# The opening of a two-block kernel: small loads moved between queues and stages, a weight slab and two memsets moved ahead

## The chip, the cores and the metric

The kernel runs on one core of a Trainium2 chip. The metric is the device time of one execution in microseconds (us), as the median of several runs.

## What is computed

Two transformer-like blocks, one behind the other, in float32, on 512 "latent" tokens and 256 context tokens of width 1024. Only the start of the first block is touched. In the reference's words:

```python
def layer_norm(x): ...                       # over the 1024 features
def ada(cvec, w, b):                         # w: 1024 x 6144
    m = jax.nn.silu(cvec) @ w + b
    return [mi[:, None, :] for mi in jnp.split(m, 6, axis=-1)]
def modulate(x, shift, scale):
    return layer_norm(x) * (1 + scale) + shift

sh1, sc1, g1, sh2, sc2, g2 = ada(c, w_ada[l], b_ada[l])
csh1, csc1, ... = ada(c_ctx[None, :], w_ada[l], b_ada[l])
u_ctx = modulate(ctx, csh1, csc1) @ w_in[l]
u_lat = modulate(x, sh1, sc1) @ w_in[l]      # w_in: 1024 x 2064
...                                          # depthwise conv, state-space scan, Fourier
                                             # mix, pooling, w_out, norm, conv FFN, then
                                             # all of the second block
```

So before the first product with `w_in`, the tokens have to be normalised and the first 2048 columns of the modulation (`sh1`, `sc1`, for both conditioning vectors) have to be there.

## The kernel before

**Layout.** Tokens lie along the free dimension, features on the 128 partitions in 8 "k-tiles" (`KT`). A norm works on 16 tiles `u`: `u` = 0 to 7 are the latent tokens (range r = 0, 512 wide), 8 to 15 the context tokens (r = 1, 256 wide).

**Weights.** All big weights come as slabs of 1024 x 256 (1 MB) through a ring of `NS` = 4 slots, in the order of the list `stream`. SyncE (SP) issues them; slab n goes into slot n % 4 and waits until slab n - 4 is used up. "Used up" is a count of `mm_done`, raised by TensorE (PE) when a unit of products is finished (`add_slabs` holds how often for each slab), or, for the slabs of `w_in`, the count `w_lo` (`split_off`): these slabs are split into a rounded part (`high`, ScalarE, ACT, line 755) and the rest (`low`, GpSimd, POOL, line 761), and once both are made from a slab its slot is free. The first slabs are 8 of `w_ada` (the modulation, "ada slabs" 0 to 7), then `w_in` 0, two more of `w_ada`, `w_in` 1, two of `w_ada`, and so on.

**The blocks.** Every `with nc.Block()` starts and ends with a barrier of all five engines.

- Block 1 (lines 1264 to 1334): SP issues the first constants, the conditioning vectors, `x` and `ctx`, then ring slabs 0 to 3, then through `load` (1268) 34 small loads (biases, gains, conv weights) and one 896 KB load of further constant matrices (`mats`). PE transposes the tokens, VectorE (DVE) and ACT copy them out of PSUM to `xT`.
- Block 2 (`units_stage`, from line 788): the norm of the tokens, the modulation, and the products with `w_in`. SP loads `wnarrow` (a 16-column piece of `w_in`) and goes on with the ring.

**The norm with its lead.** PE sums the tokens (line 436), ACT makes the mean (489), PE spreads it over the partitions (444, "mean spread"), DVE subtracts (522), ACT squares (498), PE sums the squares (436). Between them `Lead` does the first 8 ada slabs, one at every second tile `u`: PE multiplies (`ada_slab`, 621), ACT copies the result (`ada_take`, 639), PE turns it (`ada_tiles`, 630). At u = 9 PE also transposes the small parameters (1358), which needs all small loads. ACT makes the root of the variance (482; the first of them needs an activation table load), DVE its reciprocal (516), PE spreads it (444, "rstd spread" 0 for the latent, 1 for the context tokens). DVE adds the bias to the modulation (`ada_finish`, 648 and 654). From then on each tile goes through four steps on three engines: DVE multiplies (536), ACT scales and shifts (509), DVE rounds (546, "cast"), POOL subtracts to get the rest (552, "lo tile"). The products of unit group 0, the "opening" (782), go k by k: for each k-tile two units of three products, waiting for lo tile k; first all latent ones, then the context ones. Rstd spread 1 stands on PE ahead of the first product.

**Order on the other engines.** ACT makes `high` of halves 0 and 1 and the rounded narrow piece (902) behind the last root and ahead of the first step 509. POOL does `low` of halves 0 and 1, the narrow piece's rest (886), three memsets that clear the padding of the output buffers (890: 5404, 514 and 1056 columns), then the 16 lo tiles, then further `low` halves. Every engine runs its own list in order.

## Time and profile before

| | us |
|---|---|
| median of 3 runs | 2721.28 |
| lowest and highest | 2718.79, 2722.8 |
| the profiled execution: its time, and its span | 2731.0, 2729.2 |
| PE busy in the span | 2439.9 (89%) |
| DVE, POOL, ACT busy | 1210.4, 993.8, 824.2 |
| mean granted TensorE clock (share of full) | 0.932 |

The busy lines give the sum over the span. The 40 slices of the profile's page cover 68 us each, and the row of PE begins 4, 9: the first slice holds PE at 4 tenths, the second at 9 or more. The change lies within the first slice and a half. Times inside the span are counted from its start.

### The profile page before, as it was taken

To read this page: it belongs to the slowest core of one execution; us is meant where nothing else is said; L and a number is where in the kernel's file an instruction comes from. 1 tells how busy PE (TensorE), PEld (TensorE's weight loads), DVE (VectorE), ACT (ScalarE), POOL (GpSimd) and SP (SyncE) were. 2 spreads that over 40 slices of the span, in tenths; PEclk is the share of its full clock that TensorE was granted. 3 is DMA by queue.
4 is the path that set the end of the run, shared out by engine and by line. 5 is a ranking of instruction groups with operands and counts; after the bars stand their busy time and mean duration, and the time that the engine had idled before them with its cause. 6 is when DMAs were issued, how large, how long until landed. Compare 5 with 4: busy or idle time off the path is not lost. (4 is left out here: it accounts for less than half of the span.)

```text
span 2729.2 us, 35711 instructions
## 1 busy us (share of the span) xinstructions
PE 2439.9 (89%) x14567; PEld 1977.2 (72%) x14567; DVE 1210.4 (44%) x1943; ACT 824.2 (30%) x1386; POOL 993.8 (36%) x609
## 2 busy tenths in 40 slices
PE   4997788999997998767798999999989798899998
PEld 3775465777775897654586888888876587688887
DVE  3515727756554104775615323241417653333322
ACT  3232324433334223233504111121215164322221
POOL 1434333545554331211025334342425001555553
PEclk7997887999997999787798999999999898899999
DMA  8361122544442111000011224333311100122321
GB/s 266 98 218 45 41 78 78 164 145 147 146 139 64 47 62 62 1 9 1 11 52 61 94 78 139 105 112 109 124 55 55 39 1 31 62 93 93 105 95 47
DMA packets 224704, 229.99 MB, mean 84 GB/s; under 512 B 7375, under 2 KB 221219, under 8 KB 224547
## 3 DMA queue, kind: packets, MB, share of 16 engines
q1 hardware_dynamic: 224547, 227.77, 25.9%
q8 instruction: 115, 1.88, 0.3%
q14 instruction: 42, 0.34, 0.0%
HBM read 225.65 MB, written 2.10 MB: 83 GB/s over the span
## 5 line engine op out<-in xcount | busy, mean ns | idle before, releaser
L1073 POOL TENSOR_TENSOR w_lo<-ring,w_hi 128x1024 fp32r<-128x1024 f32 x128 | 306.6, 2396 | 436.2 <-ACT w_hi L1068 436.2
L1068 ACT ACTIVATE w_hi<-ring 128x1024 fp32r<-128x1024 f32 x128 | 135.9, 1063 | 744.3 <-PE ps L1132 705.9
L1851 DVE SCALAR_TENSOR_TENSOR xT<-ps,mods,xT 128x512 f32<-128x512 f32 (+1 forms) x160 | 108.3, 683 | 547.4 <-PE ps L1132 483.4
L1130 PE MATMUL ps<-hidden_hi,w_hi 128*128 128x512 f32 (+1 forms) x768 | 274.5, 357 | 5.2 <-POOL hidden_lo L2200 4.9
L1131 PE MATMUL ps<-hidden_lo,w_hi 128*128 128x512 f32 (+1 forms) x768 | 272.0, 354 | 0.0
L1132 PE MATMUL ps<-hidden_hi,w_lo 128*128 128x512 f32 (+1 forms) x768 | 271.7, 354 | 0.0
L2120 DVE SCALAR_TENSOR_TENSOR ffn_sums<-ps,cols,ffn_sums 128x441 f32<-128x441 f32 (+2 forms) x352 | 214.9, 687 | 115.5 <-ACT ffn_sums L2043 115.5
L1130 PE MATMUL ps<-h_hi,w_hi 128*128 128x512 f32 (+1 forms) x720 | 258.0, 358 | 6.8 <-POOL w_lo L1073 3.0
L1131 PE MATMUL ps<-h_lo,w_hi 128*128 128x512 f32 (+1 forms) x720 | 255.6, 355 | 0.0
L1132 PE MATMUL ps<-h_hi,w_lo 128*128 128x512 f32 (+1 forms) x720 | 255.4, 355 | 0.0
L2190 DVE TENSOR_TENSOR squares<-squares 128x512 f32<-128x512 f32 (+1 forms) x72 | 143.2, 1989 | 228.7 <-ACT squares L2176 228.7
L2066 POOL TENSOR_TENSOR ffn_w_lo<-ring,ffn_w_hi 128x1024 fp32r<-128x1024 f32 (+2 forms) x76 | 160.5, 2114 | 187.7 <-ACT ffn_w_hi L2023 187.7
L782 PE MATMUL ps<-h_hi,w_halves 128*128 128x512 f32 (+1 forms) x560 | 203.3, 363 | 0.0
L1130 PEld LDWEIGHTS ps<-hidden_hi,w_hi 128*128 128x128 f32 x768 | 145.2, 189 | 31.6 <-POOL hidden_lo L2200 7.7
L1132 PEld LDWEIGHTS ps<-hidden_hi,w_lo 128*128 128x128 f32 x768 | 145.1, 189 | 20.4
L1131 PEld LDWEIGHTS ps<-hidden_lo,w_hi 128*128 128x128 f32 x768 | 145.2, 189 | 19.4
L1130 PEld LDWEIGHTS ps<-h_hi,w_hi 128*128 128x128 f32 x720 | 136.5, 190 | 31.3 <-POOL w_lo L1073 6.1
L2023 ACT ACTIVATE ffn_w_hi<-ring 128x1024 fp32r<-128x1024 f32 (+2 forms) x76 | 71.9, 949 | 260.0 <-PE ps L2012 254.1
L1132 PEld LDWEIGHTS ps<-h_hi,w_lo 128*128 128x128 f32 x720 | 136.3, 189 | 19.1
L1131 PEld LDWEIGHTS ps<-h_lo,w_hi 128*128 128x128 f32 x720 | 136.5, 190 | 18.4
L761 POOL TENSOR_TENSOR ring_low<-ring,w_halves 128x1024 fp32r<-128x1024 f32 x34 | 81.0, 2390 | 177.8 <-ACT w_halves L755 177.8
L782 PE MATMUL ps<-h_hi,ring_low 128*128 128x512 f32 (+1 forms) x384 | 134.0, 349 | 0.0
(446 smaller groups left out, 5319.7 us busy)
## 6 DMA issues: line engine op xcount, KB each, us to landing
ring<-in_mlp_w SPq DMA_DIRECT2D x64, 1024.0 KB, 5.4
ring<-in_ada_w SPq DMA_DIRECT2D x48, 1024.0 KB, 5.3
ring<-in_w_ada SPq DMA_DIRECT2D x24, 1024.0 KB, 9.1
ring<-in_ffn_w_up SPq DMA_DIRECT2D x22, 1024.0 KB, 7.0
ring<-in_ab_w_in SPq DMA_DIRECT2D x11, 1024.0 KB, 5.2
ring<-in_ffn_w_down SPq DMA_DIRECT2D x12, 768.0 KB, 4.6
ring<-in_w_in SPq DMA_DIRECT2D x8, 1024.0 KB, 7.7
ring<-in_c_w_in SPq DMA_DIRECT2D x6, 1024.0 KB, 5.1
```

The costliest lines, as they stand in the source:

```text
L761: pool.tensor_tensor(low_half(h), ring_half(h), w_halves[:, h % 3, :, :].bitcast(F32), ALU.subtract)\
L782: ins = pe.matmul(o, stationary, moving, start=(k == 0 and i == 0), stop=(k == KT - 1 and i == 2))
L1068: act.activation(w_hi[m][:, 0:x["kt"], :], ring[:, x["n"] % NS, 0:x["kt"], m * P:(m + 1) * P], ACT.Copy).then_inc(SW["w_hi"].sem, 1)
L1073: pool.tensor_tensor(w_lo[m][:, 0:x["kt"], :], ring[:, x["n"] % NS, 0:x["kt"], m * P:(m + 1) * P], w_hi[m][:, 0:x["kt"], :].bitcast(F32), ...
L1130: pe.matmul(o, w_hi[m][:, k, :], h, start=(k == 0), stop=False)
L1131: pe.matmul(o, w_hi[m][:, k, :], l, start=False, stop=False)
L1132: ins = pe.matmul(o, w_lo[m][:, k, :], h, start=False, stop=(k == x["kt"] - 1))
L1851: return nc.vector.scalar_tensor_tensor(x, bank, column_of(gates, t * 2 + 2 * gate + r), x, ALU.mult, ALU.add)
L2023: act.activation(w_hi[i % NW][:, 0:kt, :], ring[:, n % NS, 0:kt, m * P:(m + 1) * P], ACT.Copy).then_inc(SW["w_hi"].sem, 1)
L2066: pool.tensor_tensor(w_lo[i % NW][:, 0:kt, :], ring[:, n % NS, 0:kt, m * P:(m + 1) * P], w_hi[i % NW][:, 0:kt, :].bitcast(F32), ALU.subtract)\
L2120: ins = dve.scalar_tensor_tensor(o, on_grid(ps[:, (first + m) % 4, :])[:, y0 + dy:y1 + dy, x0 + dx:x1 + dx], cols[:, CW + tap * 2 * FT + t ...
L2190: dve.tensor_tensor(sq, sq, sq, ALU.mult).then_inc(v_order.sem, 1)
```

## The change

Six edits, all in blocks 1 and 2:

1. **Small loads split up.** The 12 loads of the parameters 4 to 14 (`b_ada` to `ln2_b`) are issued by ACT, as the first thing it does in block 1. The other small loads and `mats` are issued by SP in block 2, ahead of `wnarrow` and of ring slab 4.
2. **Ring order.** `w_in` slab 0 becomes stream entry 4, between ada slabs 3 and 4. Entry 8 (ada slab 7) takes over its slot. Ada slab 7 gets five counts of `mm_done` (its own and the opening's four units), `w_in` 0 gets none. So stream entry 8 waits for `w_lo` = 2 (both halves of `w_in` 0 split), and entry 12, which follows entry 8 in slot 0, for the end of the opening; before, entry 12 waited for `w_lo` = 2.
3. **High halves and narrow piece on ACT** go to tiles u = 8, 10 and 12 of the squares.
4. **Memsets on POOL** stand ahead of `low`.
5. **Ada slab 0 on PE** stands between the token sums and the mean spread.
6. **Rstd spread 1 on PE** stands within the opening, behind the products of k = 4 (`pe_last`).

```diff
+        W["ada"], W["in_0"] = add_slabs("w_ada", 0, whole, cols_of(0, 4), 1), 4
+        add_slabs("w_in", 0, whole, [OFF_XBC], 0)
+        add_slabs("w_ada", 0, whole, cols_of(4 * SLAB, 4), [1, 1, 1, 1 + 4])
...
+                    if self.lead is not None:
+                        self.lead.pe(pe, 0)
                     for r in range(len(self.ranges)):
                         self.wait(pe, "mean", r + 1)
...
+            def pe_last(self, pe):
+                r = len(self.ranges) - 1
+                self.wait(pe, "recip", r + 1)
+                self.sig(self.spread(pe, r, rstd), "spread")
...
+                    if lead is not None:
+                        lead.sync(sp)
                     if narrow is not None:
                         sp.dma_start(wnarrow[:, :, :], ...)
...
                             for u in mine:
+                                if u == mine[0] and lead is not None and (r, k) == (0, 5):
+                                    norm.pe_last(pe)
                                 if u == mine[0]:
                                     norm.ready(pe, r, k)
...
+                    if lead is not None:
+                        for view, value in cleared:
+                            pool.memset(view, value).then_inc(S["cleared"].sem, 1)
                     for h in range(ahead):
                         low(pool, h)
...
             def _(act):
+                load_params(act, 4, 15)
                 act.wait_ge(S["c_turned"].sem, S["c_turned"].at(1))
...
+            def sync(self, sp):
+                load_params(sp, 15, len(col_rows))
+                load_rows(sp)
+                load(sp, mats[:, FIRST_MATS:N_MATS, :], ..., mats_in)
...
             def act(self, act, u):
                 if u % 2:
                     ...
+                elif u in (8, 10):
+                    self.high(u // 2 - 4)
+                elif u == 12:
+                    self.narrow_part()
```

**ACT, block 2, squares of the context tiles (u = 8 and up).** `squares` is line 498 (509 in the changed kernel), `ada_rows` is `ada_take`, `rstd` the root, `w_halves` the high halves, L902 and L920 the narrow piece. Before, from tile 12 on:

```order
L498 ACTIVATE squares<-big 128x256 [waits norm_sq_used,norm_centered] x2
L639 ACTIVATE ada_rows<-ps 128x256 [waits ada_tiles,mm_done]
L498 ACTIVATE squares<-big 128x256 [waits norm_sq_used,norm_centered] x2
L639 ACTIVATE ada_rows<-ps 128x256 [waits ada_tiles,mm_done]
L482 ACTIVATE rstd<-ps,mats 128x64 [waits norm_sq_used]
L755 ACTIVATE w_halves<-ring 128x1024 [waits slot_loaded0]
L755 ACTIVATE w_halves<-ring 128x1024
L902 ACTIVATE narrow_parts<-wnarrow 128x8x16 [waits loaded]
L509 ACTIVATE big<-big,mods,scls 128x512 [waits norm_scaled,v_order]
```

Now, from tile 8 on:

```order
L509 ACTIVATE squares<-big 128x256 [waits norm_sq_used,norm_centered]
L767 ACTIVATE w_halves<-ring 128x1024 [waits slot_loaded0]
L509 ACTIVATE squares<-big 128x256 [waits norm_sq_used,norm_centered]
L650 ACTIVATE ada_rows<-ps 128x256 [waits ada_tiles,mm_done]
L493 ACT_TABLE_LOAD
L493 ACTIVATE rstd<-ps,mats 128x128 [waits norm_sq_used]
L509 ACTIVATE squares<-big 128x256 [waits norm_sq_used,norm_centered]
L767 ACTIVATE w_halves<-ring 128x1024
L509 ACTIVATE squares<-big 128x256 [waits norm_sq_used,norm_centered]
L650 ACTIVATE ada_rows<-ps 128x256 [waits ada_tiles,mm_done]
L509 ACTIVATE squares<-big 128x256 [waits norm_sq_used,norm_centered]
L920 ACTIVATE narrow_parts<-wnarrow 128x8x16 [waits loaded]
```

The two high halves and the narrow piece have moved from behind the last root into the squares, and the first high half waits there for ring slot 0 to be filled a second time. Behind it on ACT stand the square of tile 9 and the take of ada slab 4.

**SP, start of block 2.** Before, behind the barrier:

```order
L791 DMA wnarrow<-in_w_in 128x8x16
L309 DMA ring<-in_w_ada 128x8x256 [waits mm_done] x4
L309 DMA ring<-in_w_in 128x8x256 [waits mm_done]
L309 DMA ring<-in_w_ada 128x8x256 [waits mm_done] x2
L309 DMA ring<-in_w_in 128x8x256 [waits mm_done]
L309 DMA ring<-in_w_ada 128x8x256 [waits w_lo]
```

Now, behind the 22 small loads that have come to stand there:

```order
L1287 DMA mats<-in_const_mats 128x14x128
L806 DMA wnarrow<-in_w_in 128x8x16
L312 DMA ring<-in_w_in 128x8x256 [waits mm_done]
L312 DMA ring<-in_w_ada 128x8x256 [waits mm_done] x3
L312 DMA ring<-in_w_ada 128x8x256 [waits w_lo]
L312 DMA ring<-in_w_ada 128x8x256 [waits mm_done] x2
L312 DMA ring<-in_w_in 128x8x256 [waits mm_done]
L312 DMA ring<-in_w_ada 128x8x256 [waits mm_done] x2
```

The fifth slab issued here (ada slab 7) now waits for POOL, and the small loads and `mats` stand ahead of all ring slabs of the block.

**POOL, block 2.** Before:

```order
L761 TENSOR_TENSOR in_w_low<-ring,w_halves 128x1024 [waits w_hi] x2
L886 TENSOR_TENSOR narrow_parts<-wnarrow,narrow_parts 128x8x16 [waits narrow_hi]
L890 MEMSET big 128x5404
L890 MEMSET big 128x514
L890 MEMSET big 128x1056
L552 TENSOR_TENSOR in_lo<-big,h_hi_50 128x512 [waits norm_hi] x8
L552 TENSOR_TENSOR in_lo<-big,h_hi_50 128x256 [waits norm_hi] x8
```

Now:

```order
L901 MEMSET big 128x5404
L901 MEMSET big 128x514
L901 MEMSET big 128x1056
L773 ISA
L773 TENSOR_TENSOR in_w_low<-ring,w_halves 128x1024 [waits w_hi] x2
L906 TENSOR_TENSOR narrow_parts<-wnarrow,narrow_parts 128x8x16 [waits narrow_hi]
L563 TENSOR_TENSOR in_lo<-big,h_hi_50 128x512 [waits norm_hi] x8
L563 TENSOR_TENSOR in_lo<-big,h_hi_50 128x256 [waits norm_hi] x8
```

The memsets need nothing and now stand first.

## Rows read from the trace of the kernel before

**Rows 1.** Timeline, 0 to 37 us: start, duration, engine (SPq: SP's queue), work, [idle before]

```profile
16.31 2.92 SPq L1268 DMA_DIRECT2D big<-in_b_ada  x1
...
23.39 0.30 SPq L1268 DMA_DIRECT2D big<-in_ssd_conv_w  x1
...
31.45 0.44 SPq L1268 DMA_DIRECT2D mats<-in_const_mats  x1
32.28 1.22 SPq L791 DMA_DIRECT2D wnarrow<-in_w_in  x1
...
32.33 4.84 PE L436 MATMUL ps<-xT,mats 128*32 128x128 f32 x128 [18.03 <-PEq L1264]
```

**Rows 2.** The ring's tile, 0 to 100 us: its loads from issue to landing

```profile
DMA to landing us min/median/max: 5.3/10.2/15.4
```

**Rows 3.** Windows: PE, PEld, DVE, ACT, POOL busy (instructions); then PEclk, DMA share, GB/s

```profile
46.00:50.00 4.00, 4.00 (x73) 2.86 (x76) 0.15 (x1) 3.10 (x7) 0.00 (x0) 1.00 1.04 353
...
73.50:77.20 3.70, 3.70 (x11) 2.93 (x11) 3.70 (x6) 2.12 (x3) 3.70 (x4) 0.50 0.00 0
77.20:92.20 15.00, 15.00 (x89) 13.31 (x87) 8.95 (x16) 6.59 (x11) 11.05 (x13) 0.99 0.00 1
92.20:212.00 119.80, 119.80 (x793) 94.94 (x792) 31.06 (x43) 37.06 (x66) 34.60 (x14) 0.99 0.58 185
```

**Rows 4.** Timeline, the modulation's part of block 2, 46 to 59 us

```profile
46.64 1.05 PE L621 MATMUL ps<-ring,sil 128*32 128x256 f32 x16
...
48.15 1.28 ACT L482 ACT_TABLE_LOAD   x1
...
49.45 0.37 ACT L482 ACTIVATE rstd<-ps,mats 128x128 f32<-128x128 f32 x1
...
50.88 0.41 ACT L498 ACTIVATE squares<-big 128x256 f32<-128x256 f32 x1
...
55.59 1.07 PE L621 MATMUL ps<-ring,sil 128*32 128x256 f32 x16
...
58.10 0.19 DVE L648 TENSOR_TENSOR mods<-ps,cols 128x32 f32<-128x32 f32 x1 [0.31 <-PE ps L630]
```

**Rows 5.** Timeline, from the modulation's end to the end of the opening

```profile
59.72 4.84 POOL L761 TENSOR_TENSOR in_w_low<-ring,w_halves 128x1024 fp32r<-128x1024 f32 x2 [59.27 <-ACT w_halves L755]
...
65.09 5.98 POOL L890 MEMSET big<- 128x5404 f32 x3
65.36 6.00 DVE L546 CAST h_hi<-big 128x512 fp32r<-128x512 f32 x1
...
71.04 17.10 POOL L552 TENSOR_TENSOR in_lo<-big,h_hi 128x512 fp32r<-128x512 f32 x16
...
71.87 1.97 PE L444 MATMUL ps<-rstd,mats 128*128 128x64 f32 x8 [13.63 <-DVE rstd L516]
...
73.60 0.77 PE L782 MATMUL ps<-h_hi,w_halves 128*128 128x512 f32 x1
...
83.40 0.50 DVE L546 CAST h_hi<-big 128x256 fp32r<-128x256 f32 x1
...
92.23 1.93 PE L621 MATMUL ps<-ring,sil 128*32 128x256 f32 x32
```

**Rows 6.** Groups by line and shape, 60 to 93 us: sum, mean ns, idle before

```profile
L552 POOL TENSOR_TENSOR in_lo<-big,h_hi 128x512 fp32r<-128x512 f32 x8 | 11.2, 1432 | 0.0
...
L509 ACT ACTIVATE big<-big,mods,scls 128x512 f32<-128x512 f32 x8 | 6.3, 808 | 8.7 <-DVE big L536 8.6
L546 DVE CAST h_hi<-big 128x256 fp32r<-128x256 f32 x8 | 6.2, 791 | 0.0
L552 POOL TENSOR_TENSOR in_lo<-big,h_hi 128x256 fp32r<-128x256 f32 x8 | 5.9, 777 | 0.0
...
L755 ACT ACTIVATE w_halves<-ring 128x1024 fp32r<-128x1024 f32 x3 | 3.1, 1045 | 0.0
```

**Rows 7.** Timeline, behind the opening: the issue of `w_in` 2, and a `low` half

```profile
94.22 0.37 SPq L309 DMA_DIRECT2D ring<-in_w_in  x1
...
112.19 3.64 POOL L761 TENSOR_TENSOR in_w_low<-ring,w_halves 128x1024 fp32r<-128x1024 f32 x1 [15.36 <-PE ps L782]
```

More of the change, by code:

```diff
@@ L462, in pe @@
                     c, w_ = self.packed(r)
-                    if self.lead is not None:
+                    if self.lead is not None and u:
                         self.lead.pe(pe, u)
@@ L896, in _, with narrow_part @@
                 def _(act):
-                    def first_parts():
-                        for h in range(min(3, n_halves) if lead is None else 2):
+                    def narrow_part():
+                        act.wait_ge(loaded.sem, loaded.at(16))
+                        act.activation(narrow_parts[:, :, 0:16], wnarrow[:, :, :], ACT.Copy)\
+                           .then_inc(S["narrow_hi"].sem, 1)
+                    if lead is None:
+                        for h in range(min(3, n_halves)):
                             high(act, h)
                         if narrow is not None:
-                            act.wait_ge(loaded.sem, loaded.at(16))
-                            act.activation(narrow_parts[:, :, 0:16], wnarrow[:, :, :], ACT.Copy)\
-                               .then_inc(S["narrow_hi"].sem, 1)
-                    if lead is None:
-                        first_parts()
+                            narrow_part()
                     else:
-                        lead.first_parts = first_parts
+                        lead.high, lead.narrow_part = (lambda h: high(act, h)), narrow_part
                     if post is not None:
@@ L1263, in program, with load, load_params, load_rows @@
         x_dst = lambda c, q: xT[:, 4 * q:4 * q + 4, c * CH:(c + 1) * CH]
+        def load(eng, dst, src, sem):
+            eng.dma_start(dst, src).then_inc(sem, 16)
+        def load_params(eng, first, last):
+            for (name, _), ap in zip(list(COL.items())[first:last], col_rows[first:last]):
+                at0, n, r = COL[name] - C_ROWS, ap.shape[0], 0
+                while r < n:
+                    g, p0 = divmod(at0 + r, P)
+                    m = min(n - r, P - p0)
+                    load(eng, row_in[p0:p0 + m, g, :], ap[r:r + m, :], params_in)
+                    r += m
+                    n_small[0] += 1
+        def load_rows(eng):
+            for name, src in (("swa_q", w["swa_q_norm_g_2"]), ("swa_k", w["swa_k_norm_g_2"])):
+                g, p0 = divmod(COL[name] - C_ROWS, P)
+                for half in range(2):
+                    load(eng, row_in[p0:p0 + 1, g, half * 64:half * 64 + 64], src, params_in)
+                    n_small[0] += 1
+            for dst, src in ((DT_B, w["ssd_dt_bias"][0].rearrange("a h -> (a h)")),
+                             (A_ROW, w["ssd_a_log"][0].rearrange("a h -> (a h)")),
+                             (GATE_B, w["ab_gate_b_2"][0]), (SINK, w["swa_sink_2"][0]),
+                             (D_ROW, w["ssd_d"][0])):
+                load(eng, rows[:, dst:dst + src.shape[0]], src.partition_broadcast(P), params_in)
+                n_small[0] += 1
         with nc.Block() as block:
```

61 lines of the change are left out of this document (22 added, 39 removed).

## The prediction

> **What bounds the kernel now.** I read the timeline of the opening first, from the barrier on, then the windows for TensorE's clock, then the groups for what one tile costs. Three stalls are to be seen.
>
> First, block 1 ends when SP is through with its small loads. Four ring slabs are issued by 16.3 us; the loads behind them reach to 31.9 us (31.45 + 0.44), PE has nothing to do for 18.03 us and starts the token sums at 32.33 [rows 1].
>
> Second, the modulation: ada slab 4 is multiplied at 46.64, ada slab 7 at 55.59, and the bias is added at 58.10 (call this moment F) [rows 4].
>
> Third, the way from F to the first product. POOL is busy with two `low` halves (4.84 us) and then with the memsets (5.98 us, to 71.07), and a DVE cast that starts at 65.36 lasts 6.00 us, to 71.36, where a cast elsewhere takes 0.50. So the lo tiles start at 71.04, rstd spread 1 at 71.87 and the first product at 73.60 [rows 5], 15.5 us behind F. The opening ends at 92.23 [rows 5]. From there to 212 us PE is busy for all of 119.80 us [rows 3]. So whatever moves the opening's end moves all behind it by as much, as long as nothing behind it becomes short of data. The sum is therefore made for one moment, the opening's end, 92.2 us in the profiled execution. That execution took 2731.0 us, 9.7 more than the median of 2721.28; I take the difference off the median.
>
> **The change part by part.**
>
> *Block 1 ends earlier.* All engines but SP are done at 14.3 to 15 us (PE is idle from 32.33 - 18.03 = 14.30 [rows 1]), SP at 16.3. With 0.4 us for the barrier (31.89 to 32.28 [rows 1]) block 2 starts at 16.7 instead of 32.3. ACT's 12 issues come ahead of its other work in block 1. The trace shows no issue from ACT; the nearest rows are SP's, 0.30 us one and 2.92 us one behind full queues [rows 1]. At 0.30 they take 3.6 us and are hidden, since ACT has slack until 16.3. I take that, as nothing is queued yet at the start; the 2.92 is a rival below.
>
> *But SP now has the small loads ahead of the ring.* The first, `b_ada`, took 2.92 us because the slabs' queues were full; the same stall now meets `ssd_conv_w`: 16.7 + 2.9 = 19.6. The rest, from 23.7 (behind `ssd_conv_w`) to 31.9, is 8.2 us, and `wnarrow` 1.22: SP is through at 19.6 + 8.2 + 1.2 = 29.0 and issues ring slab 4 [rows 1]. PE has used slabs 0 to 3 by about 30, so the slab isn't held by PE. Slab 4 to landing: 5.3 us at least, 10.2 in the median, which is behind other slabs [rows 2]. Here `mats` and `wnarrow` are ahead of it, one slab's worth, so I take 7.5: `w_in` 0 lands at 36.5. At 353 GB/s [rows 3] a slab takes 3.0 us, so ada slab 4 lands at 39.5. PE was ready for it at about 32: the gain of 15.6 us at the barrier has shrunk to 46.6 - 39.5 = 7.1.
>
> *From ada slab 4 to F.* Slab entry 8 now waits for both `low` halves, and these for ACT, which has other work between. After the wait PE is at the low clock: 1.05 us [rows 4] becomes 2.1, for 16 products in a window at 0.50 take double [rows 3]. So:
> - slab 4 multiplied and taken by ACT, 46.64 to 48.15 [rows 4], 1.5 and 1.0 for the clock: 42.0
> - ACT's table load 1.28, root 0.37, square 0.41 [rows 4], high half 1 1.05 [rows 6], handing over 0.1: 45.2
> - POOL `low` 1, 4.84 / 2 = 2.4 [rows 5], 0.1: 47.7. (`low` 0 is done at 40 and hidden by this.)
> - SP issues ada slab 7; all others have landed by 45.5, so 5.3 us [rows 2]: 53.0
> - from the multiplication to F: 58.10 - 55.59 = 2.5 [rows 4], 0.5 more for a clock that may be low: F = 56.0.
>
> So F comes 2.1 us earlier only. Its ends: slab 4 after 5.3 us and PE at full clock throughout give 52; slab 4 and ada slab 7 after 10.2 each give 64.
>
> *From F to the first product.* The high halves, the narrow piece, the `low` halves and the memsets are gone from here. Left are the scale row 0.4, one step 509 0.81 [rows 6], one cast 0.5 [rows 5], one lo tile 1.43 [rows 6] (1.2 if undisturbed, half a `low`), handing over 0.1 to 0.2: 3.3 us in place of 15.5. First product: 59.3. The memsets stand ahead of `low` from 16.7 to 22.7, where POOL waits for 36.5 anyway; DVE's subtractions begin at about 24. Their cover is large, so they cost nothing. Ada slab 0 ahead of the mean spread costs 1.07 us of a PE that will wait 7 us for slab 4: nothing.
>
> *The opening itself gets longer.* It took 92.2 - 73.5 = 18.7 us, with PE at 0.50 for 3.7 us and then at 0.99 [rows 3], because POOL was always ahead. Now PE starts with the first lo tile, and tiles must be made as fast as they are used. In the trace a cast ends only when POOL has ended its instruction: the 256-wide casts have a mean of 0.79 us in a stretch where one with no such wait takes 0.50 [rows 5, 6], and the cast from 65.36 waits until the memsets are over [rows 5]. Then cast k + 1 waits for lo tile k, and lo tile k + 1 for cast k + 1: they alternate. A 512-wide tile costs 1.2 + 0.4 + 0.1 = 1.7 us, against 1.43 [rows 6], a 256-wide one 0.6 + 0.3 + 0.1 = 1.0, against 0.78. Counted from the first product:
> - k = 0 to 4: nine products at the low clock take 3.7 us [rows 3], 21 more at 0.23 take 4.8: 8.5. (Lo tile 4 is there at 6.8.)
> - rstd spread 1: 1.97 at the low clock [rows 5], half of it now: 9.5
> - DVE's multiplication for tile 8 waits for this spread, and casts 6 and 7 stand behind it on DVE. 0.4 + 0.5 + 1.4 for multiplication, cast and lo tile 6, 0.2 for handing over: 12.0, while PE is done with k = 5 at 10.9. PE waits 1.1 us.
> - lo tile 7 at 13.6, its products to 15.0. The eight context tiles at 1.0 each: lo tile 15 at 13.7 + 8 = 21.7, its products to 22.5.
>
> So 22.5 in place of 18.7: the earlier spread costs some of what it gives. Opening's end: 59.3 + 22.5 = 81.8, against 92.2: **10.4 us less**.
>
> A rule of the Trainium skill bears on the alternation, though the sum is made without it. The page "SBUF — State Buffer", section "Who interferes with whom", says that a VectorE copy or cast in a 2-port mode and a GpSimd instruction exclude each other for the whole instruction. By that rule the tiles alternate as forecast here. The trace agrees in part: the cast beside the memsets lasted 6.00 us, over three memsets, not one [rows 5].
>
> *Ring entry 12* was free early, now it waits for the opening's end, and entries 13 and 14 (`w_in` 2) come behind it. `w_in` 2 was issued 2.0 us behind the opening's end (94.22 - 92.23 [rows 5, 7]); with one slab more ahead it lands 3.0 later, at most 2.0 + 10.2 + 3.0 = 15.2 behind the opening's end. POOL works on `low` 3 at 112.19 only [rows 7], 20 us behind it, held by PE. Hidden; if not, up to 3 us.
>
> **The rivals.**
>
> *B, the pipeline runs freely.* Casts slip in beside POOL at no cost, and PE sets the pace: 18.7 + 1.0 for the spread + 1.1 = 20.8; with PE warm at the ada slabs (F at 54.0): 54.0 + 3.3 + 20.8 = 78.1, 14.1 us less: 2707. For it: lo tiles at 1.43 with casts among them [rows 6]. Against it: these 1.43 hold the casts' turns already, and POOL had a backlog.
>
> *C, the DMA queue takes it.* Slab 4 lands 10.2 us after its issue (at 39.2 us in place of 36.5) and ada slab 7 also needs 10.2 in place of 5.3 [rows 2]. F is 63.6, the end 89.4: 2718.5. For it: most loads of this stretch took that long. Against it: they had three slabs ahead of them, ada slab 7 has none.
>
> *D, slower: ACT's issues hold block 1.* If each of the 12 takes 2.92 us [rows 1], ACT is at its copies at 35.8 and ends them 10 us later (its work reaches from 4.5 to 14.9 now); block 2 starts at 46.4, SP reaches slab 4 at 58.7, F is at 85.7 and the opening ends at 111.5: 19 us slower, 2740. It is slower than before when block 2 starts beyond 16.7 + 10.4 = 27.1, that is from about 1.3 us an issue on. Against it: at 0.7 us the queues hold nothing.
>
> *E, given back later.* The opening gains as forecast, but `w_in` 2 or the clock in the stretches behind costs 3 to 8 us: 2714 to 2719. The clock is 0.99 there [rows 3], which leaves little to lose there; behind 212 us nothing is changed.
>
> **How the numbers follow.** Forecast (A) 2721.3 - 10.4 = 2710.9, chance 0.50, its own range 2707 to 2715; B 0.20; C 0.13; D 0.04; E 0.13. The range has to reach from B's early end, 2704 (B with slab 4 at its quickest), to C, 2719. A measurement of this kernel can tell about 0.2% (5.4 us) from no change. Faster by more than that, below 2715.8: A nearly whole, B, a third of E, 0.48 + 0.20 + 0.04 and a part of C, together 0.76; slower: D and a rest, 0.05; within 0.2%: 0.19.
>
> **What would show it.** In the trace of the changed kernel: PE's token sums start near 17 us (if near 32 or later, ACT or SP still holds block 1: D). Ada slab 4 is multiplied near 39.5, ending an idle time of some 7 us that a DMA ends. The fifth slab issue of block 2 is near 47.7, behind POOL's second `low`. F near 56, first product near 59, the opening's end near 82. The lo tiles show idle time ahead of each that DVE's cast ends, at 1.7 us from tile to tile; if there is none, B holds. PE has a wait behind rstd spread 1 of about 1 us. PE idle between the opening's end and 200 us would speak for E. The prediction is wrong if F is later than 61, or if the first product doesn't follow within 5 us of F.

## The result

| | before | after |
|---|---|---|
| median, us | 2722.8 | 2711.77 |
| lowest and highest | 2718.79, 2731.36 | 2709.61, 2713.98 |
| profiled execution: time, span | 2731.0, 2729.2 | 2713.98, 2711.9 |
| ratio of the times, 95% interval | | 0.9948 [0.9932, 0.9964] |

The changed kernel's median is 11.0 us lower than the 2722.8 beside it, and 9.5 lower than the 2721.28 from which the forecast takes its 10.4 (2710.9 forecast). The ratio's interval allows anything from 9.8 to 18.5 us. The opening, for which the sum was made, gained only 7.8 us (92.23 to 84.47), not 10.4. Behind it 1.5 us more came from TensorE's clock; 1.7 us of the median's 11.0 no stretch of the traces accounts for. A copy of the changed kernel gave the same opening again (84.63) and a ratio of 0.9958 [0.9941, 0.9974].

**Block 1's end, SP and ACT's issues** (timeline of after: start, duration, engine, work, idle before and what ended it; to be held against [rows 1]):

```profile
0.74 0.47 ACTq L1287 DMA_DIRECT2D big<-in_b_ada  x1
...
5.65 0.34 ACTq L1287 DMA_DIRECT2D big<-in_ln_b  x1
...
16.45 2.52 SPq L1287 DMA_DIRECT2D big<-in_ssd_conv_w  x1
16.46 5.99 POOL L901 MEMSET big<- 128x5404 f32 x3 [16.01 <-POOLq L1314]
...
16.50 4.44 PE L439 MATMUL ps<-xT,mats 128*32 128x128 f32 x128 [2.47 <-PEq L1314]
...
19.99 3.09 SPq L1287 DMA_DIRECT2D big<-in_ffn_conv_w  x5
...
26.45 1.42 SPq L1287 DMA_DIRECT2D rows<-in_ab_gate_b  x1
...
29.34 0.97 SPq L806 DMA_DIRECT2D wnarrow<-in_w_in  x1
...
30.36 2.34 SPq L312 DMA_DIRECT2D ring<-in_w_in  x1
```

ACT's 12 issues are done at 5.99, the token sums start at 16.50 and PE has been idle for 2.47 us where it was idle for 18.03. SP comes to `w_in` 0 at 30.36.

**From the ring to F and to the first product** (the same view, partly of one engine alone; against [rows 4, 5]):

```profile
38.40 1.06 ACT L767 ACTIVATE w_halves<-ring 128x1024 fp32r<-128x1024 f32 x1 [7.33 <-DMA ring<-in_w_in]
...
41.44 1.94 PE L632 MATMUL ps<-ring,sil 128*32 128x256 f32 x16 [10.02 <-DMA ring<-in_w_ada]
...
45.72 1.04 ACT L767 ACTIVATE w_halves<-ring 128x1024 fp32r<-128x1024 f32 x1
...
46.84 2.36 POOL L773 TENSOR_TENSOR in_w_low<-ring,w_halves 128x1024 fp32r<-128x1024 f32 x1 [4.96 <-ACT w_halves L767]
...
49.22 2.43 SPq L312 DMA_DIRECT2D ring<-in_w_ada  x3
...
52.79 2.08 PE L447 MATMUL ps<-rstd,mats 128*128 128x128 f32 x8
...
55.01 1.93 PE L632 MATMUL ps<-ring,sil 128*32 128x256 f32 x16
...
58.60 0.19 DVE L659 TENSOR_TENSOR mods<-ps,cols 128x32 f32<-128x32 f32 x1 [1.31 <-PE ps L641]
...
59.88 0.43 DVE L557 CAST h_hi<-big 128x512 fp32r<-128x512 f32 x1 [0.16 <-ACT big L520]
60.39 1.26 POOL L563 TENSOR_TENSOR in_lo<-big,h_hi 128x512 fp32r<-128x512 f32 x1 [10.58 <-DVE h_hi L557]
60.82 1.11 DVE L557 CAST h_hi<-big 128x512 fp32r<-128x512 f32 x1
...
61.80 0.76 PE L794 MATMUL ps<-h_hi,w_halves 128*128 128x512 f32 x1 [3.06 <-POOL in_lo L563]
62.02 1.29 POOL L563 TENSOR_TENSOR in_lo<-big,h_hi 128x512 fp32r<-128x512 f32 x1 [0.36 <-DVE h_hi L557]
...
71.42 1.00 PE L447 MATMUL ps<-rstd,mats 128*128 128x64 f32 x8
...
72.45 0.42 DVE L547 TENSOR_TENSOR big<-big,ps 128x256 f32<-128x256 f32 x1 [3.93 <-PE ps L447]
...
73.29 1.27 POOL L563 TENSOR_TENSOR in_lo<-big,h_hi 128x512 fp32r<-128x512 f32 x1 [3.40 <-DVE h_hi L557]
```

Block 2 starts 15.8 us earlier, ada slab 4 is multiplied 5.2 earlier, F is 0.5 *later* than before (58.60 against 58.10). The whole gain of the opening arises between F and the first product, 3.2 us in place of 15.5; the opening itself takes 22.7 us where it took 18.6. Six of the eight 512-wide lo tiles show 0.36 us of idle time each that a DVE cast ends (the first and the seventh show 10.58 and 3.40), six of the eight 256-wide ones 0.23.

### The profile page after: what moved, and what is told of

The parts are those of the page before. It is cut to its first block and busy times, and to the rows that moved or that the text cites. A ratio compares the mean times of both kernels' runs of the same rounds, so it can differ in the third digit from the quotient of the medians.

```text
span 2711.9 us, 35711 instructions
## 1 busy us (share of the span) xinstructions
PE 2437.3 (90%) x14567; PEld 1972.6 (73%) x14567; DVE 1204.0 (44%) x1943; ACT 824.0 (30%) x1386; POOL 994.3 (37%) x609
## 5 line engine op out<-in xcount | busy, mean ns | idle before, releaser
L1890 DVE SCALAR_TENSOR_TENSOR xT<-ps,mods,xT 128x512 f32<-128x512 f32 (+1 forms) x160 | 108.1, 682 | 544.8 <-PE ps L1153 483.3
L1152 PEld LDWEIGHTS ps<-h_lo,w_hi 128*128 128x128 f32 x720 | 136.5, 190 | 18.5
L2049 PE MATMUL ps<-ffn_h_hi,ffn_w_hi 128*128 128x512 f32 x336 | 133.8, 398 | 0.0
```

The costliest lines, as they stand in the source:

```text
L1152: pe.matmul(o, w_hi[m][:, k, :], l, start=False, stop=False)
L1890: return nc.vector.scalar_tensor_tensor(x, bank, column_of(gates, t * 2 + 2 * gate + r), x, ALU.mult, ALU.add)
L2049: pe.matmul(o, w_hi[i % NW][:, k, :], hi[:, k0 + k, :], start=(k == 0), stop=False)
```

## Experiments

Where an expectation speaks of a "Theory T" or "T2", it says in brackets what that is. All times are in us. F, lo tile 0's start, the first product and the opening's end are read from the timeline of each kernel's profiled execution. The last two columns are the gain at the opening's end (against 92.23) and the gain of the median over the kernel before on the same chip.

| kernel | F | lo tile 0 | first product | end | gain at the end | gain of the median |
|---|---|---|---|---|---|---|
| before | 58.10 | 71.04 | 73.60 | 92.23 | | |
| after | 58.60 | 60.39 | 61.80 | 84.47 | 7.8 | 11.0 |
| after_again | 58.91 | 60.78 | 62.20 | 84.63 | 7.6 | 9.1 |
| e1_memsets_back | 59.35 | 61.15 | 62.56 | 85.17 | 7.1 | 10.6 |
| e2_spread_back | 58.08 | 59.96 | 65.39 | 83.81 | 8.4 | 9.2 |
| e3_small_loads_back | 60.31 | 62.18 | 63.59 | 84.90 | 7.3 | 12.5 |
| e4_memsets_alone | 60.82 | 67.77 | 71.55 | 90.44 | 1.8 | 5.0 |
| e5_warm | 60.13 | 62.01 | 63.43 | 85.55 | 6.7 | 4.1 |
| e6_ring_first | 55.56 | 57.44 | 58.85 | 81.52 | 10.7 | 13.1 |
| e7_slab_alone | 66.57 | 68.45 | 73.87 | 91.70 | 0.5 | -0.5 |
| e8_no_slab_move | 54.47 | 61.41 | 62.81 | 84.37 | 7.9 | 9.6 |
| e9_ring_ahead | 47.35 | 53.71 | 55.29 | 76.91 | 15.3 | 17.0 |
| e10_both | 50.17 | 51.95 | 53.37 | 75.72 | 16.5 | 15.5 |
| e11_two_edits | 51.08 | 58.02 | 61.81 | 80.26 | 12.0 | 12.0 |

The two last columns go together one for one, within about 5 us either way: the opening's end is the right place to make the sum for, and a single median can't say more than that about a single edit. What is said of edits therefore goes by the timelines. There is one profiled execution of each kernel, and they scatter too: between the kernels that have edit 1 whole, block 2's token sums start anywhere from 16.45 to 17.71 us, so a difference of 1 us at the opening's end is no finding.

### One edit undone

The changed kernel once more, as a measure of the scatter.

> The changed kernel once more, beside the others of this group. Opening's end at 84.5 us plus or minus 1 in the profile; 10 to 12 us less than the kernel before in the timed runs.

Its median was 2715.12 (before 2724.26), 3.4 above the first; its opening differs by 0.2.

**e1_memsets_back**: the memsets go back behind the `low` halves and the narrow piece.

```diff
-                    if lead is not None:
-                        for view, value in cleared:
-                            pool.memset(view, value).then_inc(S["cleared"].sem, 1)
...
-                    if lead is None:
+                    if True:
```

> The changed kernel with the three memsets back behind the narrow piece on POOL, as before the change; all other edits stay. Theory T (what counts between F and the first product is that the two high and two low halves are gone from there; POOL is idle from 49.8 to 60.4 us in the changed kernel): the memsets run from 49.8 to 55.8 us, hidden, F stays near 58.6, first product near 61.8, opening's end at 84.5 us plus or minus 0.5. Rival (the memsets' 6 us are part of what the change won there, as the prediction's sum has it): first product at 67 to 68, opening's end near 90.

2714.66 against 2725.22, 0.9954 [0.9934, 0.9973]. The memsets ran from 50.58 to 56.57, beside the wait for ada slab 7, and lo tile 0 came 1.8 us behind F as in after. Block 2 started 1.2 later in this execution (17.66), which is enough for the 0.7 by which the end came later. Edit 4 is worth nothing once edits 2 and 3 have taken the `low` halves out of the way.

**e2_spread_back**: rstd spread 1 goes back ahead of the first product.

```diff
-                    if (k == KT - 1 and r == last and self.lead is None) or (k == 4 and r > 0):
+                    if (k == KT - 1 and r == last) or (k == 4 and r > 0):
...
-                                if u == mine[0] and lead is not None and (r, k) == (0, 5):
-                                    norm.pe_last(pe)
```

> The changed kernel with rstd spread 1 back ahead of the first product; all other edits stay. Theory T (the early start is paid back by the wait of DVE and POOL for the spread, a POOL idle time of 3.4 us): first product near 66 instead of 61.8, no wait of POOL before lo tile 6, opening's end near 85.6 instead of 84.5. Rival (the spread held the opening back, and the move is worth its wait): opening's end 4 us later, near 88.5.

2716.0 against 2725.22, 0.9962 [0.9946, 0.9979]. The first product moved from F + 3.2 to F + 7.3, but the opening then took 18.4 in place of 22.7 us: from F to the end 25.73, against 25.87 in after. With the spread in front, POOL is through with lo tile 15 earlier (79.99), but PE has started late and sets the end; with the spread inside, PE starts early, POOL has the gap of 3.40 us ahead of lo tile 6, and the lo tiles then set PE's pace nearly to the end (lo tile 15 ends at 83.48, and PE begins its products at 83.66). The end at 83.81 is earlier than both expectations had it (85.6 and 88.5); of that, 0.5 is an earlier F. Edit 6 is worth nothing here.

**e3_small_loads_back**: SP's 22 loads and `mats` go back to block 1; ACT keeps its 12.

```diff
+                load_params(sp, 15, len(col_rows))
+                load_rows(sp)
+                load(sp, mats[:, FIRST_MATS:N_MATS, :], ..., mats_in)
...
             def sync(self, sp):
-                load_params(sp, 15, len(col_rows))
-                load_rows(sp)
-                load(sp, mats[:, FIRST_MATS:N_MATS, :], ..., mats_in)
+                pass
```

> The changed kernel with SP's 22 small loads and the constant matrices back in block 1 (the 12 of ACT stay with ACT). Block 2 then starts near 29.3 us instead of 16.5. Theory T (the start of block 2 is not what F hangs on: the ring slabs are issued behind the same small loads in either case): w_in 0 is issued near 35 and lands near 40.5, ada slab 4 is multiplied near 44, F near 59.2, opening's end near 85.1, 0.6 later than with the change. Rival (the opening follows the start of block 2): 12.8 us later, opening's end near 97.

2712.74 against 2725.22, 0.9962 [0.9947, 0.9977]. The token sums came at 27.77, 11.3 us later than in after, but ada slab 4 at 43.73, 2.3 later, F at 60.31, 1.7 later, and the end at 84.90, 0.4 later. As long as the small loads stand ahead of the ring on SP, it matters little on which side of the barrier they stand. That holds for SP's half of edit 1; the half that went to ACT was never undone by itself.

**e8_no_slab_move**: edits 2 and 3 undone, so the order of the ring, and the high halves behind the last root, are as before.

```diff
-        W["ada"], W["in_0"] = add_slabs("w_ada", 0, whole, cols_of(0, 4), 1), 4
-        add_slabs("w_in", 0, whole, [OFF_XBC], 0)
-        add_slabs("w_ada", 0, whole, cols_of(4 * SLAB, 4), [1, 1, 1, 1 + 4])
-        W["in"] = len(stream) - 1
+        W["ada"] = add_slabs("w_ada", 0, whole, cols_of(0, 8), 1)
+        W["in"] = len(stream)
...
-                elif u in (8, 10):
-                    self.high(u // 2 - 4)
-                elif u == 12:
-                    self.narrow_part()
...
+                self.high(0)
+                self.high(1)
+                self.narrow_part()
```

> The changed kernel with edits 2 and 3 undone: ada slabs 4 to 7 follow each other in the ring, w_in 0 comes behind them, high halves and narrow piece stand behind the last root again; small loads, memsets, ada slab 0 and rstd spread 1 as in the changed kernel. Theory T (edits 2 and 3 buy their shorter way from F to the opening's end with a later F, since ada slab 7 waits for POOL): ada slab 4 near 38.5, ada slab 7 near 48, F near 51.5 instead of 58.6 to 58.9, first product 8 us behind F, near 59.6, opening's end at 81 plus or minus 1.5, so 2 to 5 us earlier than with all edits. Rival (w_in 0 amid the ada slabs is what the change lives on): opening's end later than 86.

2714.2 against 2723.78, 0.9962 [0.9947, 0.9977]. F came at 54.47, 4.1 earlier, lo tile 0 at 61.41, 1.0 later, the end at 84.37, the same. Both expectations (81, and later than 86) missed. What the early high halves save behind F, they cost ahead of it: ada slab 7's load waits for POOL. Without that wait slab 7 had landed at 47.94, yet PE came to it at 51.35 only, busy throughout at the lower clock level (e11 below has the row).

### Edits alone

**e7_slab_alone**: the kernel before with edits 2 and 3 only (the diff of the ring's order and of ACT's tiles in section "The change").

> Edits 2 and 3 alone (w_in 0 amid the ada slabs, high halves and narrow piece within the squares); small loads, memsets, ada slab 0 and rstd spread 1 are as in the kernel before. Theory T (these two edits shorten the way from F to the opening's end from 34.1 to about 25.8 us, and cost on the way to F because ada slab 7 waits for the low half): block 2 starts near 32, ada slab 4 is multiplied near 48.5, F near 63.4 (5 later than before), opening's end near 89.2 instead of 92.2. Rival (the gain is spread evenly over the six edits): opening's end near 91 or later, with F to the opening's end above 30 us.

2724.79 against 2724.26, 0.9997 [0.9985, 1.0008]; F was expected at 63.4 and came at 66.57, the end at 89.2 and came at 91.70. The cost and the gain stand here side by side (timeline of e7_slab_alone, POOL's second `low`, ada slab 7, F, lo tile 0):

```profile
54.61 2.37 POOL L771 TENSOR_TENSOR in_w_low<-ring,w_halves 128x1024 fp32r<-128x1024 f32 x1 [4.96 <-ACT w_halves L765]
...
62.29 1.91 PE L630 MATMUL ps<-ring,sil 128*32 128x256 f32 x16 [2.52 <-DMA ring<-in_w_ada]
...
66.57 0.19 DVE L657 TENSOR_TENSOR mods<-ps,cols 128x32 f32<-128x32 f32 x1 [3.05 <-PE ps L639]
...
68.45 1.27 POOL L561 TENSOR_TENSOR in_lo<-big,h_hi 128x512 fp32r<-128x512 f32 x1 [5.13 <-DVE h_hi L555]
```

Ada slab 7 is there 5.3 us behind the second `low` (54.61 + 2.37 = 56.98), F is 8.5 us later than before, and F to lo tile 0 is 1.9 us in place of 12.9. Of the gain of 11.1 us, 8.5 are spent on F, and 2.1 on the way from lo tile 0 to the end (23.25 against 21.19).

**e4_memsets_alone**: the kernel before with edit 4 only.

```diff
+                    if lead is not None:
+                        for view, value in cleared:
+                            pool.memset(view, value).then_inc(S["cleared"].sem, 1)
                     for h in range(ahead):
                         low(pool, h)
...
+                    if lead is None:
```

> The kernel before with only the memsets moved ahead of the low halves. Theory T: POOL starts the lo tiles at 65.2 instead of 71.0 and no cast lasts 6 us; rstd spread 1 is done near 68.6, first product near 68.7 instead of 73.5, opening's end near 87.3 instead of 92.2: some 5 us by this edit alone. Rival (the low halves and the spread hold it anyway): opening's end stays above 91.

2720.22 against 2725.22, 0.9979 [0.9966, 0.9993]. From F to lo tile 0 it took 6.95 us in place of 12.94, the 6.0 of the memsets. At the end 4.5 of them are left (F to end 29.6 against 34.1), and F itself was 2.7 later in this execution: 1.0 since block 2 began later, and part of the rest since PE's clock was at the lower level from 55.5 (the spread ahead of ada slab 7 took 2.08 us where it took 1.16 before). The end was expected at 87.3, or above 91; it came at 90.44, between the two. Without edits 2 and 3, edit 4 shortens the way from F to the end by 4.5 us, though this execution shows only 1.8 of them at the end.

**e11_two_edits**: the kernel before with edits 1 and 4 only: `load_params(act, 4, 15)` on ACT, the other loads in `sync`, the memsets first.

> The kernel before with edits 1 and 4 alone (small loads split over ACT and block 2, memsets first); the ring order, the high halves, ada slab 0 and rstd spread 1 as in the kernel before. Theory T2: F near 54.5 to 55, first lo tile near 61.5, opening's end near 84.4, the same as with all six edits (84.5 and 84.6). Rival (the ring order or one of the small PE edits is needed for the gain): opening's end at 87 or later.

2713.46 against 2725.5, 0.9954 [0.994, 0.9969]. The end was expected at 84.4 and came at 80.26, 4.2 us earlier than in after and 10.2 earlier than in e4, which lacks only edit 1. Its span, 2706.1, is the second lowest of all. From F to the end it takes 29.2 us, 3.3 more than after, although the `low` halves alone stand for 4.8 there. Its groups by line and shape from 46 to 93 us show why it isn't more (sum, mean ns, idle before), those of after follow:

```profile
L558 POOL TENSOR_TENSOR in_lo<-big,h_hi 128x512 fp32r<-128x512 f32 x8 | 11.1, 1426 | 0.0
...
L558 POOL TENSOR_TENSOR in_lo<-big,h_hi 128x256 fp32r<-128x256 f32 x8 | 6.0, 784 | 0.0
```

```profile
L563 POOL TENSOR_TENSOR in_lo<-big,h_hi 128x512 fp32r<-128x512 f32 x8 | 10.3, 1283 | 16.2 <-DVE h_hi L557 16.2
...
L563 POOL TENSOR_TENSOR in_lo<-big,h_hi 128x256 fp32r<-128x256 f32 x8 | 5.9, 748 | 1.4 <-DVE h_hi L557 1.4
```

In e11 POOL never waits for DVE between lo tiles: while it makes the `low` halves (52.62 to 57.46), DVE gets ahead with multiplications and casts. In after it waits ahead of most. So POOL's 4.8 us of `low` behind F aren't lost entirely; they build a stock of rounded tiles.

e11 and e8 differ by edits 5 and 6 only, yet F lies 3.4 us apart. The windows name the clock (PE, PEld, DVE, ACT, POOL busy with instructions; then the share of the clock granted, DMA share, GB/s), e11 first, then e8:

```profile
45.60:57.00 11.40, 5.62 (x100) 3.94 (x88) 6.00 (x12) 7.30 (x14) 4.38 (x2) 0.91 1.10 349
```

```profile
45.60:51.00 5.40, 5.40 (x53) 3.85 (x52) 0.00 (x0) 1.52 (x4) 0.00 (x0) 0.50 1.10 349
```

e11's PE was at the upper clock level from 45.6 to 54.9 (it fell again before 57, hence the mean of 0.91), e8's stayed at the lower until 52.5. Why, no run tells. Edit 5 moves one product group and wasn't tried alone. But the level can differ without any edit ahead of it: e2 is the same program as after up to the last ada slab, and its ada slab 6 took 1.05 us where after's took 1.93. So the 4.2 us between e11 and after are no clean measure of edits 2, 3, 5 and 6.

### What holds F

**e5_warm**: 14 products of 512 columns, which nobody uses, ahead of tile 8 on PE, to keep the clock up while PE waits for ada slab 4.

```diff
+                if u == 8:
+                    for _ in range(14):
+                        pe.matmul(ps[:, 2, :], ident, xT[:, 0, 0:LAT], start=True, stop=True)
```

> The changed kernel with 14 matmuls of 512 columns on PE between tiles 7 and 8 (their result goes into a PSUM bank that is overwritten before it is read), in the stretch in which PE waits from 31.4 to 41.4 us for ada slab 4. The granted clock is then at its upper level when ada slab 4 comes, a slab takes 1.07 instead of 1.93 us on PE. Theory T (F hangs on the way ada slab 4, take, root, high half 1, low half 1, load of ada slab 7, of which PE's speed is only the first step): F at 56.4 to 57.5 instead of 58.6, PE waits for the DMA of ada slab 7, opening's end near 83. Rival (PE at its lower clock sets the pace from ada slab 4 on, the low half and the load come in time): 11.5 us from ada slab 4 to F as in the kernel before, F near 53, opening's end near 79.

2720.17 against 2724.26, 0.9983 [0.9973, 0.9993]: 5 us slower than after_again beside it. The fill took 12.28 us and delayed ada slab 4 to 43.26. PE's clock was at the upper level when slab 4 came, but ada slab 7 came no sooner (timeline of e5_warm):

```profile
48.43 1.07 PE L632 MATMUL ps<-ring,sil 128*32 128x256 f32 x16
...
55.83 1.94 PE L632 MATMUL ps<-ring,sil 128*32 128x256 f32 x16 [4.20 <-DMA ring<-in_w_ada]
```

Ada slab 6 takes 1.07 where after needs 1.93, and then PE waits 4.20 us for a DMA, which was issued when POOL's second `low` was done (50.16). F came at 60.13, expected from 56.4 to 57.5. In after the chain high half, `low` half, load is the floor under F, and the slow clock lies only a little above it: slab 7's load took 5.4 us and landed at 54.6, and PE, still busy with the spread of 52.79 at the lower level, began slab 7 at 55.01. In e2, where the level rose at ada slab 6, PE waited for the load instead and F came 0.5 us earlier (timeline of e2_spread_back):

```profile
54.43 1.28 PE L632 MATMUL ps<-ring,sil 128*32 128x256 f32 x16 [2.25 <-DMA ring<-in_w_ada]
```

So a better clock alone is worth about half a microsecond at F in this order of the ring. Of the 5 us of the median the opening explains 0.9; the rest wasn't found.

**e6_ring_first**: after, with `w_in` 0 and ada slab 4 ahead of the rest on SP.

```diff
+                load_slabs(sp, 5)
                 load_rows(sp)
+                load_slabs(sp, 6)
                 load(sp, mats[:, FIRST_MATS:N_MATS, :], ..., mats_in)
```

> The changed kernel with two ring issues moved ahead on SP: w_in 0 goes out behind the conv and gain parameters, ada slab 4 behind the row loads, and the constant matrices and the narrow piece come after. Theory T (F hangs on when w_in 0 and ada slab 4 land, and that on the small loads ahead of them on SP): w_in 0 is issued near 24 instead of 30.4 and ada slab 4 near 28.5; ada slab 4 is multiplied near 34 instead of 41.4, F near 51, opening's end near 77, 7 us earlier than with the change. Rival (the small loads and the constant matrices, now late, hold tile 9, the narrow piece or the last ada tiles): F stays at 57 or later.

2711.17 against 2724.26, 0.9947 [0.9932, 0.9961]. Expected was F near 51 and an end near 77; they came at 55.56 and 81.52, the end 3 us earlier than in after. The next wait had taken over (timeline of e6_ring_first):

```profile
30.69 3.32 SPq L806 DMA_DIRECT2D wnarrow<-in_w_in  x1
...
34.72 1.93 PE L632 MATMUL ps<-ring,sil 128*32 128x256 f32 x16 [2.97 <-DMA ring<-in_w_ada]
...
42.62 1.94 PE L632 MATMUL ps<-ring,sil 128*32 128x256 f32 x16 [2.74 <-DMA ring<-in_w_ada]
```

Ada slab 4 came 6.7 us earlier. Ada slab 5 stood on SP behind `mats` and `wnarrow`, whose issues now took 1.43 and 3.32 us with two slabs still in flight, where they took 0.44 and 0.97.

**e9_ring_ahead**: e8 with the whole ring ahead. SP issues entry 4 before the row loads, entries 5 to 8 before `mats` and `wnarrow`. The narrow piece (ACT and POOL) goes behind the norm, and PE waits for `mats` behind the opening only.

```diff
                 load_params(sp, 15, len(col_rows))
+                load_slabs(sp, 5)
                 load_rows(sp)
+                load_slabs(sp, 9)
                 load(sp, mats[:, FIRST_MATS:N_MATS, :], ..., mats_in)
...
                 elif u == 15:
-                    pe.wait_ge(mats_in, 16)
...
                     norm.pool(pool)
+                    if narrow is not None and lead is not None:
+                        narrow_low()
```

> The kernel of e8_no_slab_move, and on SP ring entry 4 goes out behind the conv and gain parameters, entries 5 to 8 behind the row loads, the constant matrices and the narrow piece behind them; the narrow piece is split behind the norm (ACT behind the last step of the norm, POOL behind the last lo tile), and PE waits for the constant matrices behind the opening instead of at tile 15. Theory T (the opening hangs on the order in which SP's queue brings ada slabs 4 to 7 and w_in 0, nothing else of the change): ada slab 4 near 32, F near 45, first product near 51 to 53, opening's end at 71 to 75, some 10 us earlier than with the change; 2700 to 2705 us timed where the kernel before has 2724. Rival (something else, POOL's low halves or the small parameters for tile 9, holds it): opening's end at 79 or later.

2706.83 against 2723.78, **0.9936 [0.9923, 0.995]**: the lowest median of all, 5 us below after. Timeline of e9_ring_ahead, from ada slab 5 to the first product:

```profile
35.13 1.07 PE L629 MATMUL ps<-ring,sil 128*32 128x256 f32 x16 [0.59 <-DMA ring<-in_w_ada]
...
39.18 1.94 PE L629 MATMUL ps<-ring,sil 128*32 128x256 f32 x16 [2.09 <-DMA ring<-in_w_ada]
...
47.35 0.19 DVE L656 TENSOR_TENSOR mods<-ps,cols 128x32 f32<-128x32 f32 x1 [0.49 <-PE ps L638]
...
48.89 4.85 POOL L770 TENSOR_TENSOR in_w_low<-ring,w_halves 128x1024 fp32r<-128x1024 f32 x2 [26.18 <-ACT w_halves L764]
53.71 4.28 POOL L560 TENSOR_TENSOR in_lo<-big,h_hi 128x512 fp32r<-128x512 f32 x3
...
55.29 0.77 PE L791 MATMUL ps<-h_hi,w_halves 128*128 128x512 f32 x1 [7.80 <-POOL in_lo L560]
```

F is 10.8 us earlier than before; the `low` halves are back behind F, and still the opening ends at 76.91. The expected 71 to 75 were missed since ada slabs 5 and 6 still waited for their loads and the opening took 21.6 us.

**e10_both**: after with e9's order on SP, both high halves at u = 8, and the narrow piece and the wait for `mats` moved as in e9.

> The changed kernel with SP's order mended (ring entry 4, w_in 0, behind the conv and gain parameters, entries 5 to 8 behind the row loads, constant matrices and narrow piece behind them), both high halves one behind the other at tile 8, the narrow piece split behind the norm, PE's wait for the constant matrices behind the opening. Theory T2 (in all kernels so far the opening ends 23 to 24 us behind the start of the first lo tile where nothing is stocked up, and the lo tiles start 1.8 us behind F once the low halves are out of the way; F hangs on the load of ada slab 7 behind low half 1): low half 1 ends near 37, F near 46.5, first lo tile near 48.3, opening's end near 72, 12.5 us earlier than with the change and 5 earlier than e9_ring_ahead; 2698 to 2703 us timed where the kernel before has 2724. Rival (w_in 0 amid the ada slabs costs as much as it gives in this order too, as it did in e8_no_slab_move): opening's end near 77, as in e9_ring_ahead.

2710.05 against 2725.5, 0.9941 [0.9923, 0.9958]; the end at 75.72, expected 72. F came at 50.17, not 46.5. With `low` done at 37.75, PE waits for no DMA ahead of ada slabs 5, 6 and 7; slab 7's load, issued at 37.78, took 6.0 us, and PE came to it at 47.06 (timeline of e10_both):

```profile
38.42 1.93 PE L632 MATMUL ps<-ring,sil 128*32 128x256 f32 x16
...
41.66 1.93 PE L632 MATMUL ps<-ring,sil 128*32 128x256 f32 x16
...
44.84 2.08 PE L447 MATMUL ps<-rstd,mats 128*128 128x128 f32 x8
...
47.06 1.67 PE L632 MATMUL ps<-ring,sil 128*32 128x256 f32 x16
```

Here, where loads are early, the low clock is what is left. Its opening ended 1.2 us before e9's; its median isn't lower, and the intervals overlap. Of the two, e9 needs fewer of the edits. e9 without edits 5 and 6, which e11 suggests, wasn't tried.

## The prediction, step by step

- **Block 1's end: right.** Token sums at 16.50 (16.7 forecast). ACT's issues took 0.28 to 0.65 us each and 5.3 us together, where the sum had 3.6. They are hidden all the same: SP's slab issues, to 16.05, still end block 1. Rival D (2.92 us each) is out. The Trainium skill's page "DMA: Bandwidth & Descriptors", section "Issuing engines are not separate DMA queues", says that starting DMAs on several engines saves only the sequencers' time to issue them. The trace agrees: what edit 1 freed on SP in block 1 was issue time, and the loads left to SP met the same full queues (2.52 us for `ssd_conv_w`).
- **SP to slab 4: 1.4 short.** Forecast 29.0, measured 30.36: one of the five issues of `ffn_conv_w` took 1.56 us, and `gate_b` 1.42, where each took 0.43 in the kernel before. The landing took 0.5 more. Ada slab 4 was multiplied at 41.44, not 39.5: 1.9 late.
- **From ada slab 4 to the load of ada slab 7: the mechanism right**, and 0.4 us quick. The second `low` ended at 49.20, SP issued at 49.22.
- **Ada slab 7 to F: mis-sized.** The load was right (5.4 us, 5.3 forecast), but PE began slab 7 0.4 us behind its landing, and the "0.5 more for a clock that may be low" wasn't enough: from 41.4 to 56.9 every ada slab took 1.93, and from slab 7's multiplication to F it took 3.6 where 3.0 were forecast. Together F is 2.6 late (1.9 - 0.4 + 0.1 + 0.4 + 0.6), and 0.5 behind the F of before. The sum counted the lower level for slab 4 and, by way of caution, behind slab 7; it lasted through all four slabs, although PE was busy nearly all of that time (window of after: PE, PEld, DVE, ACT, POOL, then the granted share of the clock):

```profile
41.40:57.40 16.00, 15.96 (x141) 9.83 (x141) 3.33 (x7) 6.38 (x14) 3.30 (x3) 0.50 0.81 259
```

- **F to the first product: right** (3.2, forecast 3.3), but not for the reason given for each part. The prediction let the memsets' move carry 6 of the 12 us. e1 shows that with edits 2 and 3 in place it carries nothing, and e4 that without them it carries 6.0.
- **The length of the opening: right** (22.7, forecast 22.5), and by its chain: tiles at 1.64 and 0.97 from start to start (62.02 - 60.39 = 1.63; forecast 1.7 and 1.0), each behind a cast. The spread came at first product + 9.6 (71.42 - 61.80), not + 8.5, since the low clock lasted from 61.8 to about 67.6 and not 3.7 us, and lo tile 6 ended at + 12.8, not + 12.0. PE waited 0.75 us for lo tile 6 in the matmul rows, 1.1 forecast. The delay was made good by the last three tiles, which came back to back (0.70 and 0.75 us from start to start, 1.0 forecast), and by the rest at 0.97: lo tile 15 ended at + 21.7, as forecast. The length is thus right to 0.2 us in part by luck, as two errors of about 0.8 us cancel. Rival B, a free pipeline, is out.
- **The end: 2.7 late**, 84.47 against 81.8, all of it from F.
- **Behind the opening: right but for the clock.** "Whatever moves the opening's end moves all behind it by as much." PE is busy from the opening's end on, as forecast. Yet the next gap moved by more, 220.67 to 211.41, 9.3 us (rows of before, then of after; PE idle of 8.03 in both):

```profile
220.67 5.51 PE L374 MATMUL ps<-mats,big 128*128 128x128 f32 x33 [8.03 <-PEq L1468]
```

```profile
211.41 5.56 PE L377 MATMUL ps<-mats,big 128*128 128x128 f32 x36 [8.03 <-PEq L1507]
```

1.5 us more came in one window, where before ran at the lower level and after didn't (windows of before, then of after):

```profile
108.00:112.00 4.00, 4.00 (x23) 4.00 (x22) 4.00 (x9) 0.00 (x0) 0.00 (x0) 0.57 0.00 0
```

```profile
108.00:112.00 4.00, 4.00 (x46) 3.48 (x48) 1.64 (x4) 0.98 (x2) 0.79 (x2) 1.00 0.00 0
```

All kernels agree on this price: from the opening's end to the product group behind that gap it takes 128.4 us in the eight that have such a fall of the clock (listed under the hardware), and 126.9 to 127.0 in the six that have none. So the step itself held to a tenth of a microsecond, and the 1.5 us are a term that the sum didn't have: rival E looked behind the opening for a loss only, on the ground that the clock of 0.99 left little to lose.

Behind 220 us nothing of the program is changed, and the profiled spans differ by 8 us more. In the median 11.0 - 9.3 = 1.7 are left, in the copy's 9.1 nothing. The granted clock in later stretches differs from kernel to kernel (0.88 and 0.90 from 215 to 600 us, 0.83 and 0.87 from 1200 to 1500, before and after), and no run ties this to the change.

So the total of 10.4 was met partly by luck: 1.5 us from the clock and 1.7 us that nothing accounts for stood in for the 2.7 us that F was late. Rivals C (F at 63.6) and E (`w_in` 2 late, which wasn't: PE had no gap from 80 to 200 us) are out.

And the larger miss is one of design, which no rival held: the prediction gave most of the gain to edits 2, 3 and 6. e11 has 12.0 us at the opening's end from edits 1 and 4 alone; e7 has 0.5 from edits 2 and 3, e4 1.8 from edit 4. The larger part hangs on edit 1, and e3 shows that SP's half of it carries little once the others are in place.

## What to carry to other kernels

When work is taken off the path behind a moment by putting it ahead of it, ask what then waits for that work. A ring slot that is freed by a split makes the split's engines a part of the load's path. Price each edit with and without the others, since two that hide the same stall pay once. And where the next stage works tile by tile through several engines, an engine that starts late may lose nothing, as it starts on a stock.

## What the runs showed of the hardware

- **One dip of the clock keeps to one place of the program, and comes in some kernels only.** Before, PE fell to the lower level at about 108.1 us, 0.6 us after 2.5 us of narrow products (eight of 2 columns and twelve of 16 columns), and was back at 111.5. A fall of the same kind was there in e4 and e7 (from about 107), e3 (101), e8 (100), e2 (99.5), e11 (96) and e9 (93), each time 15 to 16 us behind the opening's end; from 93 to 121 us all eight have the same mean of 0.94. It was missing in after, its copy, e1, e5, e6 and e10, with 1.00 over that stretch, although the same narrow products are there (97.3 to 99.7 in after). So these products alone don't bring it. It is no matter of edit 2, which e2, e3 and e7 have too. What decides it stays open; it costs 1.5 us.
- **PE can stay at the lower level while it works without a break.** In after it was busy for 15.96 of 16.00 us with 141 products, four ada slabs of 256 columns and much narrower ones between them, at a granted clock of 0.50. In e11 the level rose amid the same work at 45. Where loads are early this sets F (e8 and e11 lie 3.4 us apart), where a load comes late it is worth 0.5.
- **A cast and POOL alternate, with a gap**: beside lo tiles the 512-wide cast takes 1.1 us (60.82 in after) where one with POOL idle takes 0.43 (59.88), and POOL idles 0.36 us per tile. The page "SBUF — State Buffer" of the Trainium skill, section "Who interferes with whom", has a VectorE cast in a 2-port mode and a GpSimd instruction exclude each other for the whole instruction; these rows agree with it, one tile against one cast, though none says which mode the cast is in.
- **An issue behind slabs in flight costs the issuer, and the cost moves with the order.** `wnarrow`, 128 x 8 x 16, took 0.97 us to issue in after, where no slab was in flight, and 3.32 in e6, 4.16 in e10 and 5.18 in e9, where two were. `mats` took 0.44 with none in flight, 0.59 (e10) and 1.43 (e6) with two, and 4.08 (e9) with three.
